# RWKV-7 stage of a diffusion backbone: the input load of the group five ahead, issued before the wait for the inverted blocks instead of behind the spreading

## What is computed

```python
def step(s, inp):
    w_t, k_t, v_t, kk_t, a_t = inp[:5]
    sa = jnp.einsum('bhvk,bhk->bhv', s, kk_t)
    s = (s * w_t[:, :, None, :] - sa[..., None] * (kk_t * a_t)[:, :, None, :]
         + v_t[..., None] * k_t[:, :, None, :])
    y = jnp.einsum('bhvk,bhk->bhv', s, inp[5])
    return s, y
```

## Time and profile before

| | |
|---|---|
| median of 3 runs | 6016.99 us (6013.84 to 6020.24) |
| the profiled execution | 6029.24 us, first to last instruction 6027.3 us |
| granted TensorE clock, mean | 0.949 |
| PE busy | 5344.6 us (89%) |
| DVE busy | 2668.9 us (44%) |
| ACT busy | 1743.2 us (29%) |
| POOL busy | 1329.3 us (22%) |
| DMA of the queue that SP issues | 495.75 MB, 28.3% of 16 engines |
| the stage `rwkv` | 3602 to 5720 us |

### The profile page before, as it was taken

One profiled execution on the slowest core, in us unless ns is written; L12 is line 12 of the kernel. 1 busy time (PEld: TensorE's weight loads), 2 busy tenths in 40 slices (PEclk: granted clock), 3 DMA queues, 4 the chain that ended last, 5 costly groups with the idle time before them and its releaser, 6 DMA issues. The chain is left out here.

```text
span 6027.3 us, 138697 instructions
## 1 busy us (share of the span) xinstructions
PE 5344.6 (89%) x56750; PEld 3286.3 (55%) x56750; DVE 2668.9 (44%) x4658; ACT 1743.2 (29%) x4007; POOL 1329.3 (22%) x2745
## 2 busy tenths in 40 slices
PE   7999997999999879999999986888888888888879
PEld 1666662333333235444444435777777777777834
DVE  0333335666666422222232224555545545455466
ACT  0222112443434303221122112333333333333322
POOL 0001102222222100000000003444444443344333
PEclk9999998999999989999999997999999999998989
DMA  6122211000000253221111213333343333433375
GB/s 246 58 66 67 62 55 44 21 21 22 21 21 21 111 209 138 75 72 52 64 64 60 66 60 89 87 86 88 92 96 87 86 87 89 96 89 86 71 241 181
DMA packets 774893, 503.67 MB, mean 84 GB/s; under 512 B 509248, under 2 KB 726976, under 8 KB 767296
## 3 DMA queue, kind: packets, MB, share of 16 engines
q1 hardware_dynamic: 774336, 495.75, 28.3%
HBM read 312.10 MB, written 183.50 MB: 82 GB/s over the span
## 5 line engine op out<-in xcount | busy, mean ns | idle before, releaser
L1534 PE MATMUL p_bU<-keep_hT,p_slab 128*128 128x512 f32 (+1 forms) x2592 | 1029.2, 559 | 12.7 <-DMA p_slab<-in_o_w_in_dram 7.2
L1534 PEld LDWEIGHTS p_bU<-keep_hT,p_slab 128*128 128x128 f32 x2592 | 493.1, 191 | 543.7 <-issue 512.3
L883 PE MATMUL at_bS<-at_qT,at_kT 97*64 97x512 f32 (+1 forms) x2368 | 602.1, 598 | 7.4 <-issue 6.8
L1015 DVE TENSOR_REDUCE at_mx<-at_bM 128x1 f32<-128x512 f32 (+1 forms) x656 | 400.5, 629 | 354.0 <-PE at_bM L849 351.0
L978 ACT ACTIVATE at_pT<-at_bS 128x512 f32<-128x512 f32 (+1 forms) x592 | 346.9, 591 | 462.1 <-PE at_bS L883 384.3
L2291 DVE SCALAR_TENSOR_TENSOR rw_S<-rw_bank,rw_dec,rw_Sdec 128x64 f32<-128x64 f32 x576 | 136.5, 278 | 668.5 <-PE rw_bank L2047 668.5
L1606 DVE SCALAR_TENSOR_TENSOR p_z<-p_u,p_shift,p_z 128x2306 f32<-128x2306 f32 x26 | 68.2, 2621 | 769.8 <-ACT p_z L1564 769.8
L1870 POOL TENSOR_TENSOR rw_g_at<-rw_g_at,rw_g_prod 64x14 f32<-64x14 f32 (+6 forms) x1008 | 332.8, 330 | 79.0
L1904 PE MATMUL rw_bank<-rw_lin,rw_wl 64*64 64x256 f32 x1152 | 114.0, 527 | 251.7 <-DMA rw_lin<-scratch_lora 215.5
L1868 POOL TENSOR_TENSOR rw_g_prod<-rw_g_at 64x14 f32<-64x14 f32 (+6 forms) x1008 | 312.6, 310 | 79.1
L883 PEld LDWEIGHTS at_bS<-at_qT,at_kT 97*64 97x64 f32 x2368 | 161.1, 138 | 267.2 <-issue 215.0
(11 more groups left out here) (266 smaller groups left out, 10056.6 us busy)
## 6 DMA issues: line engine op xcount, KB each, us to landing
rw_zin<-scratch_heads SPq DMA_DIRECT2D x144, 512.0 KB, 5.0
mod_w<-in_ada_w_dram SPq DMA_DIRECT2D x4, 6144.0 KB, 18.3
scratch_heads<-p_z SPq DMA_DIRECT2D x24, 1024.0 KB, 4.9
rw_lin<-scratch_lora SPq DMA_DIRECT2D x144, 128.0 KB, 5.3
scratch_bv<-rw_bv SPq DMA_DIRECT2D x144, 128.0 KB, 2.0
scratch_products<-rw_NB SPq DMA_DIRECT2D x288, 64.0 KB, 2.2
rw_XB<-scratch_inverses SPq DMA_DIRECT2D x288, 64.0 KB, 2.4
scratch_y<-rw_ysb SPq DMA_DIRECT2D x288, 64.0 KB, 3.5
```

Of the source, the lines that this page charges most:

```text
L883: last = pe.matmul(bS[rows, g % 3, 0:nq * P], kT[:, s, k * P + VH * x:k * P + VH * x + VH], qT[:, s, q0 * P:(q0 + nq) * P], start=True, st ...
L1015: nc.vector.tensor_reduce(mx[:, j, piece:piece + 1], bM[:, (FIRST_ITEM[b] + i) % 2, 0:n], AX.X, ALU.max).then_inc(max_red, 1)
L1534: last = pe.matmul(bU[:, n % 4, 0:w], slab[:, i, k, :], hT[:, k, tok:tok + w], start=(k == 0), stop=(k == KD - 1))
```

## The change

In SP's body the two lines of `load` move from behind `spread` (ahead of `gather`) to behind `store_bonus` (ahead of `keep_inverses`). The same DMAs are issued, the same semaphores are waited for, and no other engine's program changes.

```diff
 def body(n, has):
     if has[3]:
         store_bonus(n.on(3))
+    if has[5] and n.since(-3):
+        load(n.on(5))
     if has[2]:
         keep_inverses(n.on(2))
     if has[3]:
         keep_products(n.on(3))
     if has[2]:
         spread(n.on(2))
-    if has[5] and n.since(-3):
-        load(n.on(5))
     if has[3]:
         gather(n.on(3))
     if has[0]:
         store_y(n)
```

## The result

| | before | after |
|---|---|---|
| median | 6018.61 us (4 runs, 6013.84 to 6023.31) | 5604.49 us (4 runs, 5601.37 to 5610.96) |
| first to last instruction, profiled | 6027.3 us | 5599.6 us |
| ratio after to before | | 0.9313, 95% interval 0.9297 to 0.9329 |
| granted TensorE clock, mean | 0.949 | 0.974 |
| PE busy | 5344.6 us | 5207.7 us |

The kernel is 6.9% faster, 414 us by the medians and 428 us by the two profiles. All of it lies in the stage `rwkv`: up to the first store of inverted blocks the two profiles differ by 4 us, behind the 70th by 5 us the other way.

The account below looks back on a forecast made before the run. The closed loop of SP and POOL was taken to set the 29.02 us turn. Issue 2.67 and landing 2.9 us leave it, 70 x 5.57 = 390 us saved, giving 5627 us; range 5575 to 5775 us.

Parts of the forecast that it names:

- rival A: The forecast itself: loop and PE nearly balanced, turn 22.8 to 24.4 us, 5584 to 5694 us; chance 0.62.
- The bound before: SP and POOL wait for each other in a closed loop filling the 29.02 us turn; PE only follows.
- The issue, 2.67 us: On SP, issuing the load's four DMAs leaves the path from inversion to gather: 2.67 us a turn.
- The landing, 2.9 us: Without the load's 1.28 MB in front, the gather lands in 2.4 us instead of 5.3: 2.9 us.
- The inversion, left as it was: POOL's inversion, 13.61 us in the turn shown, was assumed to keep its length.
- Rival B: POOL's inversion gets slower by meeting DVE's work: 1.6 us come back, turn 25.05, 5739 us; chance 0.25.
- The sum: Turn is the longer of loop 23.45 and PE 22.83 us: 5.57 us saved in each, 390 us in all.
- What is late next: PE's body without its waits for `rw_lin` and `rw_r` is the next floor: 22.83 us a turn.
- The cover: The moved load's issue lands in SP's wait for POOL: 13.1 us of cover, about 5 to spare afterwards.
- Rivals C, D and E: C: only issue saved, 5830 us, chance 0.07; D: PE's chain bounds, 6017 us, 0.04; E: slower, 6087 us, 0.02.

Follow-up runs that it names:

- small DMAs early: Kernel before, with only the load's two small DMAs (`lin`) moved ahead of the inverses' store under their own semaphore; 5897.21 us.
- shorter inversion: Kernel before, with four of the 14 elimination steps of POOL's inversion left out; 5798.89 us.
- less work on PE: Kernel before, with 48 of PE's matmuls left out in each body (`second_w`, `higher_orders` over one chunk of four); 6009.16 us.
- load behind the gather: Kernel before, with the load moved directly behind the gather, ahead of the outputs' store; 5587.48 us.
- large DMAs early: Kernel before, with only the load's two large DMAs (`zin`) moved ahead of the inverses' store; 5773.3 us.
- blank issues: Changed kernel, with four DMAs of 4 bytes issued at the load's old place behind the spreading; 5712.83 us.

## Why the prediction was right

The median, 5604.49 us, lies in the range, 22.5 us under the forecast of 5627; the forecast's own range, 5584 to 5694, holds it too. The change came out as rival A, at the very edge of its 22.8 to 24.4 us a turn. The mechanism was right; that the number is so near is partly luck, since the terms were off by up to 1.0 us in both directions. By its steps:

- **The bound before** was the loop of SP and POOL, as read from the earlier trace rows. Shown: the small DMAs early freed PE of its wait for them and gave no more than the loop did; the shorter inversion gave all of its time; less work on PE gave 0.2 us.
- **The issue, 2.67 us.** The time from the end of the spreading to the gather's issue, in the mean of 61 turns, was 3.45 us before and 0.10 after: 3.35. The term was too small by 0.7 us, for two reasons. I took the shown turn, in which no issue was held up, while in other turns one takes up to 2.35 us: in 54 of the 61 turns the mean was 3.11 before. And once for each pair of heads `load` issues eight DMAs, not four, with the weights `rw_wl` among them: in these 7 turns it was 6.17.
- **The landing, 2.9 us.** `rw_g_at` needed 5.3 us before and 2.8 at the median after: 2.5 us. The two late turns without a load told it nearly right; it was over-sized by 0.4 us.
- **The inversion, left as it was.** This was the mis-sized term. I left it at its old length; it shrank by 1.0 us, from 12.98 to 11.98, the largest of the four misses. The rows had a sign of it: in the late turn without load only 12.75 us lie between the last gather issue and the store, against 18.9, and these 6.15 are more than the 2.9 that I gave to the landing. POOL's inversion there ran from 5676.89 to 5687.76, 10.87 us with no key arithmetic beside it, where the shown turn has 13.61; I took the landing from that turn and not the inversion. Rival B had asked the right question, what VectorE work the inversion will lie on, and answered it the wrong way: it newly meets little, since `rw_Kc`, `rw_Bc` and the two `rw_AR` (4507.94 to 4511.84 in the turn shown) are over before it starts at 4513.30, and it leaves the key arithmetic behind. The rule of the Trainium skill cited there (SBUF — State Buffer, Who interferes with whom) fits what was measured: `rw_b`, with two SBUF inputs, took 1644 ns when POOL's `rw_cx` had started 0.5 us before it, and 693 at most in the run with the load behind the gather.
- **The sum.** 3.35 + 2.54 (from the last gather issue until POOL starts, 4.77 before and 2.23 after in the mean) + 1.00 are 6.9 us; the remaining issues of SP took 0.7 us longer in the mean (products 3.81 for 3.57, spreading 3.21 for 2.99, gather 1.39 for 1.10), which leaves 6.1 of the 6.20 measured. The forecast had 5.57, and held these other issues for unchanged.
- **What is late next.** PE, at 22.83 us by my working, 22.3 by the window of a body with nothing but the fixed wait. I had subtracted the two waits from 26.90, but PE's busy time fell too, from 22.49 to 21.95: 0.5 us, which I had not subtracted; why it fell no run separates. That the measured turn of 22.82 equals my 22.83 is chance: it is made of 22.3 and small waits. That the changed kernel runs on PE's body plus a toll, and not on the loop at 23.45, is where the forecast's picture was off.
- **The cover.** SP still waits 5.5 us a turn for POOL (381.5 us in 69), close to the 5 forecast. Rivals C, D and E found nothing: no landing of 5 us, no PE bound before, no SP that comes later than POOL.

## What to carry to other kernels

When two engines each wait for the other a large part of a period, add up the pieces from the one to the other and back: if they fill the period, every instruction on that path may count in full, a DMA issue with its 0.6 us as much as the transfer that stands in front of a small one the loop waits for. Full pieces are not yet the proof: before the change 3.4 us less of inversion gave 3.3 us a turn, after it 2.9 us less gave 0.57, because another engine stood right behind. Take a piece out and look. Move what nobody in the loop waits for to where the queue idles. After that the length of an engine's work may change because it lies beside other work, so ask in which part of the new period it will lie before leaving its duration as it was.

## What the runs showed of the hardware

- A gather of 64 KB right behind 1.0 MB (small DMAs early) or 1.28 MB (before) of loads in SP's queue landed in 5.2 and 5.3 us at the median; without the large loads in front of it, in 2.4 to 2.8 (large DMAs early, blank issues, behind the gather, changed).
- Issuing a DMA of 4 bytes kept SP for 0.34 us, one of 128 or 512 KB for about 0.6 us, now and then for up to 2.35 (before); why is not known.
- PE's granted clock in the steady stretch was 0.92 with 4.2 us of waits a turn for `rw_lin` and `rw_r` (before) and with 3.4 for `rw_r` (small DMAs early), 0.96 with 2.2 for both (large DMAs early), 0.97 with 1.4 for `rw_r` (blank issues), and 1.00 in the changed kernel, which has neither. PE's busy time in a turn fell from 24.0 to 22.0 us from before to changed.
- Beside POOL's `rw_cx`, which started 0.5 us before it, VectorE's `rw_b` of 0.69 us took 1.64 us (changed).
